# Sparse attention with unnormalised queries: one factor per token and head on the logits, key panels first, selection rounds dealt differently

## What is computed

```python
aq = apply_rope(rmsnorm_2(aq.reshape(B, T, 8, 64), q_norm[l]), cos, sin)
ak = apply_rope(rmsnorm_2(ak.reshape(B, T, 8, 64), k_norm[l]), cos, sin)
...
score = einsum('bqh,bqhs->bqs', wi, relu(einsum('bqhd,bsd->bqhs', qi, ki)))   # -inf where not visible
_, idx = lax.top_k(score, 128)
logits = einsum('bqhd,bqkhd->bhqk', q, k_sel) * 64 ** -0.5
p = softmax(logits)
```

## Time and profile before

| | us |
|---|---|
| median of 3 runs | 2621.76 (2620.92 to 2625.23) |
| the profiled execution, its own time | 2622.3 |
| its span | 2620.5 |
| PE busy in the span | 2550.2 (97%) |
| DVE busy | 1154.1 (44%) |
| ACT busy | 991.8 (38%) |
| POOL busy | 1086.2 (41%) |
| TensorE's granted clock over the span | 0.995 of full speed |

### The profile page before, as it was taken

One profiled execution on the slowest core, in us unless ns is written; L12 is line 12 of the kernel. 1 busy time (PEld: TensorE's weight loads), 2 busy tenths in 40 slices (PEclk: granted clock), 3 DMA queues, 4 the chain that ended last, 5 costly groups with the idle time before them and its releaser, 6 DMA issues.

```text
span 2620.5 us, 30123 instructions
## 1 busy us (share of the span) xinstructions
PE 2550.2 (97%) x12440; PEld 2085.7 (80%) x12440; DVE 1154.1 (44%) x1977; ACT 991.8 (38%) x1128; POOL 1086.2 (41%) x816
## 2 busy tenths in 40 slices
PE   7999999999999999999999999999999999999999
PEld 5887778878888787877788888888787778888887
DVE  6352353365424466987434111124698743411112
ACT  4523533343323454635434222235463543422220
POOL 4333334544545443213354444444421326444442
PEclk9999999999999999999999999999999999999999
DMA  4222222222222232212123322232221212222222
GB/s 161 80 80 66 88 73 81 97 97 91 98 98 95 85 97 69 73 50 79 49 97 97 97 97 97 97 97 84 81 73 58 72 49 97 97 97 97 97 97 81
DMA packets 210611, 226.81 MB, mean 87 GB/s; under 512 B 4545, under 2 KB 200347, under 8 KB 210347
## 3 DMA queue, kind: packets, MB, share of 16 engines
q1 hardware_dynamic: 209968, 224.74, 27.0%
q10 hardware_dynamic: 507, 0.15, 0.0%
HBM read 217.01 MB, written 2.10 MB: 84 GB/s over the span
## 4 chain that ended last, share of the span: by engine, by line
PE 79%; DVE 14%; ACT 4%; issue 1%; DMA 1%; POOL 0%; SPq 0%; DVEq 0%; ACTq 0%
PE psum L487 71%; PE psum L770 1%; PE psum L782 1%; PE psum L759 1%; ACT wh L1043 1%; DVE top L2084 1%; PE psum L641 1%; DVE attT L1758 1%; DVE ul L1949 1%; DVE score L2086 1%; DVE dec L1744 1%; DVE normed L1700 1%; DVE merged L1972 1%; DVE tmp L1836 1%; DVE tmp L1838 0%
## 5 line engine op out<-in xcount | busy, mean ns | idle before, releaser
L1613 POOL TENSOR_TENSOR wl<-raw,wh 128x512 fp32r<-128x512 f32 x812 | 1086.0, 1371 | 1510.6 <-ACT wh L1043 1373.1
L487 PE MATMUL psum<-uh,wh 128*128 128x512 f32 x2016 | 801.6, 398 | 9.7 <-DVE ul L1639 3.0
L487 PE MATMUL psum<-uh,wl 128*128 128x512 f32 x2016 | 787.8, 391 | 0.0
L487 PE MATMUL psum<-ul,wh 128*128 128x512 f32 x2016 | 787.5, 391 | 0.0
L1043 ACT CAST wh<-raw 128x2048 fp32r<-128x2048 f32 (+1 forms) x206 | 387.0, 1880 | 298.9 <-DMA raw<-in_w_ffn_out 119.1
L487 PEld LDWEIGHTS psum<-uh,wh 128*128 128x128 f32 x2016 | 379.7, 188 | 97.2 <-issue 12.8
L487 PEld LDWEIGHTS psum<-uh,wl 128*128 128x128 f32 x2016 | 379.5, 188 | 80.4
L487 PEld LDWEIGHTS psum<-ul,wh 128*128 128x128 f32 x2016 | 380.0, 188 | 77.7 <-issue 2.4
L487 PE MATMUL psum<-fh,wh 128*128 128x512 f32 x528 | 205.9, 390 | 0.0
L487 PE MATMUL psum<-fh,wl 128*128 128x512 f32 x528 | 205.7, 390 | 0.0
L487 PE MATMUL psum<-fl,wh 128*128 128x512 f32 x528 | 205.7, 390 | 0.0
(11 more groups left out here) (353 smaller groups left out, 3350.6 us busy)
## 6 DMA issues: line engine op xcount, KB each, us to landing
raw<-in_w_in SPq DMA_DIRECT2D x78, 1024.0 KB, 5.3
raw<-in_w_ffn_in SPq DMA_DIRECT2D x44, 1024.0 KB, 5.1
raw<-in_w_up SPq DMA_DIRECT2D x22, 1024.0 KB, 5.0
raw<-in_w_ffn_out SPq DMA_DIRECT2D x16, 1024.0 KB, 5.1
raw<-in_w_down SPq DMA_DIRECT2D x8, 1024.0 KB, 5.2
raw<-in_w_out SPq DMA_DIRECT2D x8, 1024.0 KB, 5.1
raw<-in_w_ffn_out SPq DMA_DIRECT2D x8, 768.0 KB, 4.4
raw<-in_w_o SPq DMA_DIRECT2D x4, 1024.0 KB, 5.2
```

Source lines behind the costliest of these rows:

```text
L487: ins = mm(dst, x, y, start=first and i == 0, stop=last and i == len(todo) - 1)
L1613: ins = nc.gpsimd.tensor_tensor(wl[p % 3][:, w], raw[p % 3][:, w], wh[p % 3][:, w].bitcast(F32), ALU.subtract)
```

## The change

The keys are projected first (j = 0, 1), the queries after them (j = 2, 3). Keys are normalised as before. Queries are rotated and multiplied by their gain, but not by the inverse root of their mean square. For j = 2, 3 PE sums the squares with the data as the stationary operand and two columns of `blk` as the moving one: eight matmuls of two columns that give [token, head] instead of [head and value, token]. ACT takes the mean of those 16 columns for j = 2 and nothing else; for j = 3 it takes the mean of 16 more, then logarithm, exponential and square of all 32 columns. DVE makes `rq` (128 x 32) of them in two instructions, and L1892 takes its column as scale in place of 1.0. The rounds of token tile 1 are dealt (3, 3, 5, 5) over units 3 to 6, and none is done in unit 7.

```diff
-                  C_IK, C_IQ, C_AQ, C_AQ + 256, C_AK, C_AK + 256, C_AV, C_AV + 256, C_HG, C_HG + 256):
+                  C_IK, C_IQ, C_AK, C_AK + 256, C_AQ, C_AQ + 256, C_AV, C_AV + 256, C_HG, C_HG + 256):
...
-SELECT_UNIT, SELECT_CORE, SELECT_POST = (0, 0, 0, 4, 3, 3, 3, 3), (8, 8), 5
+SELECT_UNIT, SELECT_CORE, SELECT_POST = (0, 0, 0, 3, 3, 5, 5, 0), (8, 8), 5
...
-        small = sb("small", [P, 64])
+        small = sb("small", [P, 88])
...
+        rq = small[:, 55:87]
+        head_cols = blk.rearrange("p (e d) -> p e d", d=HD)[:, :, 0]
...
-        qk_pair = [aq[:, 0:2, :], aq[:, 2:4, :], ak[:, 0:2, :], ak[:, 2:4, :]]
+        qk_pair = [ak[:, 0:2, :], ak[:, 2:4, :], aq[:, 0:2, :], aq[:, 2:4, :]]
...
                     for i in range(2):
-                        ins = mm(dst[:, i, :], blk, qksq[:, i, :], start=True, stop=True)
+                        if j < 2:
+                            ins = mm(dst[:, i, :], blk, qksq[:, i, :], start=True, stop=True)
+                        for m in range(NT if j >= 2 else 0):
+                            at = 4 * m + 2 * i
+                            ins = mm(dst[:, 0, at:at + 2], qksq[:, i, m * P:(m + 1) * P], head_cols, start=True, stop=True)
...
-                    if j > 0:
-                        act.wait_ge(S.r_normed, t.up(S.r_normed))
-                    else:
+                    if j == 0:
                         act.wait_ge(S.rope_done, t.up(S.rope_done))
                         t.up(S.rope_done, 4)
+                    elif j < 3:
+                        act.wait_ge(S.r_normed, t.up(S.r_normed))
+                    if j >= 2:
+                        x, y, yy = (b[:, 0, 0:8 * NT] for b in (tmp[1], tmp[0], tmp[3]))
+                        mean_square(x[:, 4 * NT * (j - 2):4 * NT * (j - 1)], src[:, 0, 0:4 * NT], 1.0 / HD, pair_free[mean % 2])
+                        if j == 3:
+                            act.wait_ge(pair_free[mean % 2], mean // 2 + 1)
+                            logarithm(y, x)
+                            inverse_root(y, yy).then_inc(S.r_root, 1)
+                        return
...
-                            ins = v.tensor_tensor_reduce(out=logit[:, e, 0:kk], in0=X[e][:, 0:kk], in1=mask, scale=1.0,
+                            at = 4 * NT * (p // 2) + 4 * m + 2 * (p % 2) + e
+                            ins = v.tensor_tensor_reduce(out=logit[:, e, 0:kk], in0=X[e][:, 0:kk], in1=mask, scale=rq[:, at:at + 1],
...
                 def normed(j):
+                    if j == 2:
+                        return
                     dve.wait_ge(S.r_root, t.up(S.r_root))
+                    if j == 3:
+                        x, y, yy = (b[:, 0, 0:8 * NT] for b in (tmp[1], tmp[0], tmp[3]))
+                        v.scalar_tensor_tensor(yy, yy, -1.0, x, ALU.mult, ALU.mult).then_inc(S.dve_chain, 1)
+                        dve.wait_ge(S.dve_chain, t.up(S.dve_chain))
+                        v.scalar_tensor_tensor(rq, yy, 3.0, y, ALU.add, ALU.mult).then_inc(S.r_normed, 1)
+                        dve.wait_ge(S.r_normed, t.up(S.r_normed))
+                        return
```

More of the change, by code:

```diff
@@ L1230, in logarithm, with inverse_root @@
                 act.wait_ge(S.act_chain, t.up(S.act_chain))
-            def inverse_root(y):
+            def inverse_root(y, square=tmp[3][:]):
                 fn(y, y, ACT.Exp, scale=-0.5).then_inc(S.act_chain, 1)
                 act.wait_ge(S.act_chain, t.up(S.act_chain))
-                return fn(tmp[3][:], y, ACT.Square)
+                return fn(square, y, ACT.Square)
             def silu_gate(dst, cast=True):
@@ L2151, in cosines @@
                     x = qk_pair[j]
-                    v.scalar_tensor_tensor(x, x, gains_of(l)[j // 2], cosT[:].unsqueeze(1).to_broadcast([P, 2, T]),
+                    v.scalar_tensor_tensor(x, x, gains_of(l)[1 - j // 2], cosT[:].unsqueeze(1).to_broadcast([P, 2, T]),
                                            ALU.mult, ALU.mult).then_inc(S.dve_chain, 1)
@@ L2198, in side_core_2 @@
                     next_pair()
-                    sine(50 + 2 * l + j // 2, 4)
+                    sine(51 + 2 * l - j // 2, 4)
                     yield
@@ L2293, in _ @@
             for l in range(LAYERS):
-                v.tensor_scalar(small[:, 9 + l:10 + l], vech[:, V_QN + l:V_QN + l + 1], -HD ** -0.5, None, ALU.mult).then_inc(S.dve_chain, 1)
+                v.tensor_scalar(small[:, 9 + l:10 + l], vech[:, V_QN + l:V_QN + l + 1], HD ** -0.5, None, ALU.mult).then_inc(S.dve_chain, 1)
                 dve.wait_ge(S.dve_chain, t.up(S.dve_chain))
```

## The result

The changed kernel takes 2626.07 us (median of 14 executions, 2622.32 to 2633.01), the kernel before 2621.89 in the same comparison (14 executions, 2618.52 to 2625.23). The ratio is 1.0016, 95% interval 1.0009 to 1.0023: 4 us slower, where 6 us faster was forecast. The profiled execution took 2628.12, its span 2626.3, at a clock of 0.995.

The account below looks back on a forecast made before the run. PE, busy 97%, bounds the kernel, so only its removed idle time counts. Unit terms give 2.9 us in layer 0, rounded to 3, two layers 6: 2622.3 to 2616.3, less 0.5 is 2615.8; own range 2613 to 2619, 8 in 10 2608 to 2621.

Parts of the forecast that it names:

- C: Rival, 7%: narrow matmuls' stationary changes do not overlap, up to 4.5 us more on PE per j; 2634, slower.
- Unit 3: Recurrence stage, layer 0: one selection round fewer, so PE's wait of 1.32 us falls to 0.34, minus 0.98.
- Unit 4: Sine product meets POOL's earlier low part, plus 0.9; the unit gives back 0.98 and costs about 0.7 us more.
- rival A: 25%: unit 4's sine product precedes POOL's first piece, nothing given back; 4.9 us a layer, 2608 to 2612.
- Units 5 and 7: PE's waits go: both in unit 5, minus 0.96 us, and the one in unit 7, minus 0.34.
- Unit 6: PE's stall for `attT` falls from 4.5 to 2.3 us; `attT` comes 2.5 earlier in all.
- The bound it named: Unit 6: rectified keys, behind a cast awaiting its panel's landing, come at about 1125.9; DVE would want them at 1125.4.
- DVE's own work in unit 6: `normed(3)` minus 3.7, two small instructions at 0.25 each, two rounds plus 1.97, admission 0.3: 1.0 us earlier.
- PE itself: Per j, sixteen short matmuls at 0.12 us replace four of 512 columns: 1.9 us either way, no change.
- The two instructions for `rq`: DVE in unit 6: two new instructions on 32 columns, put at 0.25 us each with their waits.
- The scale as a column: L1892 in the attention: costed at nothing; up to 0.05 us for each of 128, 6 us, would have to appear unhidden.
- I count no gain of clock: Unit 6's remaining stall of 2.3 us exceeds the 1.90 that preceded the lower clock in unit 1: no gain.

Follow-up runs that it names:

- pad96: Kernel before with only `small` widened from 64 to 88 columns, unused, moving the arena 96 bytes: 2637.23 us, ratio 1.0059.
- rq_home: Changed kernel with `small` back at 64 columns and `rq` in columns 0 to 31 of `vech`: 2611.78 us, ratio 0.996; repeat 2612.34, 0.9962.
- low_after_pairs: rq_home with POOL's low part in unit 4 held until DVE has copied the scores into `attT`: 2610.19 us, ratio 0.9946; repeat 2609.6.
- both32: Kernel before with an unused 32-byte tile ahead of the weight ring, moving ring and arena but not `uh`, `ul`: 2652.98 us, ratio 1.0114.
- both64: Kernel before with an unused 64-byte tile ahead of the weight ring, moving ring and arena but not `uh`, `ul`: 2654.04 us, ratio 1.0117.
- pad32: Kernel before with only `small` widened to 72 columns, unused, moving the arena 32 bytes: 2637.45 us, ratio 1.0055.
- weights32: Kernel before with the weight ring moved 32 bytes and `small` 8 columns shorter, so the arena stays: 2667.36 us, ratio 1.0169.
- pad64: Kernel before with only `small` widened to 80 columns, unused, moving the arena 64 bytes: 2627.68 us, ratio 1.0018.

## Why the prediction was wrong

**The step that failed** is one that the prediction doesn't have. It went through the removed passes, the added ones, the rounds and the narrow matmuls, and gave no term to `small` growing by 24 columns, which the diff shows. It argued PE's own work as "No change" from the narrow matmuls alone. In place of that nothing the runs put 15 us (pad96), on matmuls all over the program. None of its rivals held it either: C, the only slower one, had PE pay, but at L902. The section ahead of the prediction calls the first block untouched; its matmuls read the arena too and slow down with the rest.

**The account.** The change without the move gains 10 us (rq_home and its repeat, 10.5 and 9.7); the move costs 15 (pad96). The ratios multiply to 0.996 x 1.0059 = 1.0019, where the changed kernel has 1.0016.

**What it had right**, by its own steps:
- Unit 3: 0.34 forecast, 0.33 measured.
- Unit 4: "a new wait of 1 to 2 us before L653", beside a sine product of 2.2: 1.44 and 1.58 measured, the first beside one of 2.35. Where POOL is held away the product takes 1.28 and most of the wait goes (low_after_pairs and its repeat, layer 0). Layer 1 of rq_home shows what rival A had described: the product gets in first.
- Units 5 and 7: no waits, as forecast.
- Unit 6: 2.3 forecast, 1.93 measured. The bound it named, the rectified keys behind the cast, appears as DVE's longest wait there: 0.59 for `tmp`, after 0.20 for `dec`. (The terms it gives for DVE's own work in unit 6 add up to 0.9, not 1.0; the forecast doesn't hang on it.)
- PE itself: 1.9 us a j forecast for the narrow matmuls, 1.92 measured.

```profile
1077.65 1.92 PE L908 MATMUL psum<-const,qksq 128*128 128x2 f32 x16
```

- The two instructions for `rq` take 0.19 each, 0.45 together with their waits; 0.50 was put.
- The scale as a column: L1892's group of 48 goes from a mean of 556 to 615 ns as L1907, 0.06 a piece for the 0.05 named. For all 128 that would be 7.6 us if nothing hid it. But from the attention's start in layer 0 to the recurrence stage of layer 1 rq_home takes 630.0 us (1201.61 to 1831.66), as before (630.0): it is hidden.

**The term that was too small** is the clock: "I count no gain of clock". The granted clock in 15 us that begin 3 to 4 us before the end of unit 6's stall, layer 0 and layer 1, is shown here for before and then for rq_home (length, PE, PEld, DVE, ACT, POOL, clock, DMA).

```profile
1132.00:1147.00 15.00, 11.06 (x69) 11.07 (x70) 11.64 (x32) 1.41 (x2) 0.67 (x1) 0.77 0.00 1
1984.00:1999.00 15.00, 12.05 (x78) 11.84 (x79) 12.13 (x36) 3.19 (x3) 0.00 (x0) 0.89 0.07 11
```

```profile
1130.00:1145.00 15.00, 13.08 (x88) 12.70 (x87) 11.89 (x33) 2.95 (x3) 1.17 (x1) 0.89 0.05 8
1975.00:1990.00 15.00, 13.00 (x95) 12.36 (x94) 12.88 (x34) 3.29 (x3) 1.38 (x2) 1.00 0.15 40
```

0.77 for 15 us is 3.4 us of full clock missing, 0.89 is 1.7. Before lost 3.4 and 1.7, rq_home 1.7 and nothing: 3.4 us of clock came back in all. These are rq_home's waits in units 4 and 6, layer 0 and then layer 1:

```profile
1088.72 0.49 PE L655 MATMUL psum<-attT,gv 128*128 128x128 f32 x2 [1.56 <-DVE attT L1772]
...
1133.15 0.55 PE L655 MATMUL psum<-attT,gv 128*128 128x128 f32 x2 [1.92 <-DVE attT L1772]
```

```profile
1934.22 0.49 PE L655 MATMUL psum<-attT,gv 128*128 128x128 f32 x2 [0.37 <-DVE attT L1772]
...
1978.38 0.49 PE L655 MATMUL psum<-attT,gv 128*128 128x128 f32 x2 [2.00 <-DVE attT L1772]
```

With 0.33 in each unit 3, rq_home's units 3 to 7 have 3.81 and 2.70 of waits, for 7.14 and 7.41 before: minus 8.0, where 6 were forecast. With the clock that is 11.4; 1.3 goes back where, in that execution, unit 3 of layer 0 begins with a wait of 1.97 instead of 0.67. The sum is 10.1. The traces have 9.6: from the stage's first wait to the first attention matmul that waits, 223.9 us become 221.1 in layer 0, and 220.5 become 213.6 in layer 1. The spans differ by 10.9, because rq_home's trace is 1.3 ahead already where the first stage begins, in code that the edit leaves alone.

In the changed kernel's trace the waits are minus 7.0 (3.70 and 3.85), and unit 6 has the same clock as in rq_home. But layer 1's stage begins with two stretches at the lower clock that before doesn't have, where before has 1.00 in both windows:

```profile
1838.00:1853.00 15.00, 13.04 (x67) 11.06 (x66) 8.17 (x25) 6.51 (x8) 8.60 (x7) 0.89 0.36 118
1875.00:1890.00 15.00, 13.10 (x55) 10.24 (x54) 10.50 (x14) 3.65 (x4) 9.41 (x7) 0.89 0.10 22
```

They take back 3.4 us; in layer 0, 1.7 comes back, from 980 to 990, where the clock is 1.00 for 0.83 before. What brings them is not shown. The arena's matmuls, up to 20.7 us, turn the gain round.

The prediction held that a stall of 1.90 brought the lower clock in unit 1, so a remaining stall of 2.3 would too. In rq_home a stall of 2.00 in layer 1 was followed by a full clock, one of 1.92 in layer 0 was not. Stall length alone doesn't decide it. The trace of before could have told: in unit 1 of layer 1 nearly the same stall is followed by a full clock. The row and the window of before:

```profile
1873.04 0.71 PE L653 MATMUL psum<-attT,gv 128*128 128x128 f32 x4 [1.89 <-DVE attT L1758]
```

```profile
1870.00:1885.00 15.00, 13.09 (x64) 9.71 (x62) 11.47 (x18) 5.34 (x6) 9.35 (x7) 1.00 0.21 66
```

## What to carry to other kernels

- A tile that grows moves every tile behind it. Before a small buffer is enlarged, see what lies behind it and keep the streamed operands of each matmul a multiple of 256 bytes from their weights, the only distances that ran at full pace here (128 was not tried). Where the addresses would have to move, put the new values elsewhere, as rq_home does, or pad the tile up to such a multiple (not tried here).
- When a local edit is measured, compare the page's groups that it doesn't touch as well. Here the edited stage gained and 3096 untouched matmuls lost, each about 7 ns; mean durations of untouched groups show it in one look.
- When two engines disturb each other at a place, a hold that orders them is worth trying before the work is shortened further. Here its medians are 1.6 and 2.7 us lower, which the intervals don't yet tell from nothing.

## What the runs showed of the hardware

- 512-column fp32 matmuls of the arena run at 226.7 ns from start to start while both operands are a multiple of 256 bytes apart, also when both are moved by 32 or 64 together (before, both32, both64). With 32 or 96 bytes more (pad32, pad96), or 32 less (weights32), they run at 233.3 to 233.4 on average, 3% slower. In the changed kernel, at 96 bytes, the loss is uneven: means of 399, 394 and 393 for the three products. At 64 bytes it is 229.0 (pad64) or, for `uh` and `ul`, 233.3 (both64).
- The cost is only on PE's matmuls. The load groups keep 187 to 189 ns in every page, and the `f` groups have 0.0 of idle time before them, fast or slow.
- A two-operand DVE instruction took 2.35 when POOL's low part began 0.01 us behind it, and 1.28 when POOL began 0.05 behind it; then POOL's first piece took 2.38 for the usual 1.27. The Trainium skill (SBUF — State Buffer, "SBUF: two separate sides") has it that whichever instruction starts first gets the shared ports and the loser blocks until it ends. The second case agrees. In the first one the loser was blocked too, but by the recorded starts it was DVE that came first, so at 0.01 us the rows don't bear out who wins.
